# Norm sums carried through the residual update: added on VectorE, rooted as token columns, spread back by a matmul

## The reference

```python
def rms(x):
    xf = x.astype(jnp.float32)
    return (xf * lax.rsqrt(jnp.mean(xf * xf, axis=-1, keepdims=True) + EPS)).astype(x.dtype)
def modulate(h, shift, scale):
    return h * (1 + scale) + shift
def swiglu(h, wi, wo):
    g, u = jnp.split(h @ wi, 2, axis=-1)
    return (jax.nn.silu(g) * u) @ wo
```

## Time and profile before

| | us |
|---|---|
| median of three runs | 3114.03 |
| the profiled execution, its own time | 3109.35 |
| its span | 3107.6 |
| PE matmul busy | 2909.2 (94%) |
| DVE busy | 1670.3 (54%) |
| ACT busy | 1223.8 (39%) |
| POOL busy | 250.8 (8%) |

### The profile page before, as it was taken

How to read it: one execution, slowest core, us unless ns; L and a number is a source line. 1 busy time by engine, 2 the same in 40 slices (tenths; PEclk the granted TensorE clock), 3 DMA queues, 4 the chain that set the end, 5 groups by cost and what they waited for, 6 DMA issues and landing times.

```text
span 3107.6 us, 47235 instructions
## 1 busy us (share of the span) xinstructions
PE 2909.2 (94%) x16044; PEld 2390.0 (77%) x16044; DVE 1670.3 (54%) x2799; ACT 1223.8 (39%) x1983; POOL 250.8 (8%) x163
## 2 busy tenths in 40 slices
PE   6799998999889999899998889999799899999999
PEld 2488886764478888788886369997699899888888
DVE  0433325956443332433327546558669877677765
ACT  1322223335332222322224445445545455455444
POOL 0100002200010000100003000000028400000000
PEclk8799999999899999999999899999999999999999
DMA  7422221237222222222222344553156555566654
GB/s 290 163 100 96 95 101 69 74 128 292 95 81 95 101 95 102 81 94 96 100 102 82 136 154 159 182 203 123 69 177 213 174 172 174 186 241 240 243 206 142
DMA packets 144828, 444.84 MB, mean 143 GB/s; under 512 B 16089, under 2 KB 44889, under 8 KB 144225
## 3 DMA queue, kind: packets, MB, share of 16 engines
q1 hardware_dynamic: 112896, 409.51, 37.8%
q10 hardware_dynamic: 31840, 34.13, 3.1%
HBM read 428.37 MB, written 15.20 MB: 143 GB/s over the span
## 4 chain that ended last, share of the span: by engine, by line
PE 84%; DVE 8%; DMA 3%; ACT 2%; issue 1%; POOL 1%; SPq 0%; ACTq 0%; DVEq 0%
PE bank L1385 20%; PE bank L1386 20%; PE bank L1387 20%; PE bank L1756 11%; DMA raw<-w_stream_dram 3%; PE bank L1412 2%; PE bank L1728 2%; PE bank L1576 1%; PE bank L1617 1%; DVE stage_rs L875 1%; PE bank L1423 1%; PE bank L1450 1%; DVE cand L1186 1%; PE bank L1608 1%; PE bank L1588 1%
## 5 line engine op out<-in xcount | busy, mean ns | idle before, releaser
L1385 PE MATMUL bank<-H,w_hi 128*128 128x256 f32 (+1 forms) x3232 | 1093.2, 338 | 64.9 <-DVE H L866 58.4
L843 DVE TENSOR_TENSOR w_lo<-raw,w_hi 128x1024 fp32r<-128x1024 f32 x584 | 714.7, 1225 | 685.3 <-ACT w_hi L435 676.3
L1386 PE MATMUL bank<-H,w_hi 128*128 128x256 f32 (+1 forms) x3232 | 1068.0, 330 | 0.0
L1387 PE MATMUL bank<-H,w_lo 128*128 128x256 f32 (+1 forms) x3232 | 1067.4, 330 | 0.0
L435 ACT ACTIVATE w_hi<-raw 128x1024 fp32r<-128x1024 f32 x628 | 660.1, 1052 | 239.1 <-PE bank L1387 208.3
L1385 PEld LDWEIGHTS bank<-H,w_hi 128*128 128x128 f32 x3232 | 623.3, 193 | 136.4 <-issue 71.8
L1386 PEld LDWEIGHTS bank<-H,w_hi 128*128 128x128 f32 x3232 | 623.4, 193 | 59.5 <-issue 5.6
L1387 PEld LDWEIGHTS bank<-H,w_lo 128*128 128x128 f32 x3232 | 622.5, 193 | 54.9
L1385 PE MATMUL bank<-act_hi,w_hi 128*128 128x512 f32 (+1 forms) x704 | 263.8, 375 | 0.0
L1387 PE MATMUL bank<-act_hi,w_lo 128*128 128x512 f32 (+1 forms) x704 | 255.5, 363 | 0.0
L1386 PE MATMUL bank<-act_lo,w_hi 128*128 128x512 f32 (+1 forms) x704 | 255.5, 363 | 0.0
(11 more groups left out here) (207 smaller groups left out, 2775.8 us busy)
## 6 DMA issues: line engine op xcount, KB each, us to landing
raw<-w_stream_dram SPq DMA_DIRECT2D x772, 512.0 KB, 3.3
gelu_scratch<-gelu ACTq DMA_DIRECT2D x108, 128.0 KB, 3.5
gelu_in<-gelu_scratch ACTq DMA_DIRECT2D x108, 128.0 KB, 3.4
bias<-bias_in_dram ACTq DMA_DIRECT2D x1, 3072.0 KB
X<-x_in_dram SPq DMA_DIRECT2D x1, 2048.0 KB, 13.8
mem<-mem_in_dram SPq DMA_DIRECT2D x1, 1024.0 KB, 9.9
rope<-rope_in_dram ACTq DMA_DIRECT2D x2, 512.0 KB
sub<-sub_in_dram ACTq DMA_DIRECT2D x1, 1024.0 KB
```

The costliest lines, as they stand in the source:

```text
L843: nc.vector.tensor_tensor(w_lo[:, s, :], raw[:, s, :], w_hi[:, s, :].bitcast(F32), ALU.subtract).then_inc(lo_ready, 1)
L1385: nc.tensor.matmul(to, w_hi[:, s, cut], hi, start=first, stop=False, skip_group_check=True)
L1386: nc.tensor.matmul(to, w_hi[:, s, cut], lo, start=False, stop=False, skip_group_check=True)
L1387: return nc.tensor.matmul(to, w_lo[:, s, cut], hi, start=False, stop=last, skip_group_check=True)
```

## The change

Three things, in all seven norms with carried sums.

First, the squares of the eight chunks are no longer multiplied by `ones` one by one. ACT writes the first square to `x_sq_sum` (in `stage_rs`) and the others to two buffers in turn; DVE adds the squares of chunks 1 to 6 to it (`add_square`), the one of chunk m-1 between the split and the update of row `m`. Square 7 is not added. The loops of these rows are written out on all three engines, and PE waits for `x_done` before it reuses a bank.

Second, at the end PE takes the sum and the last square as stationary operands, one block of 128 tokens at a time, against two columns of `ones`: the sums then stand with tokens on the partitions, 8 columns (LC) or 4 (L). ACT roots these columns, DVE inverts them, and PE multiplies a broadcast of each column with the identity into bank 5, which gives the inverse root of every token on all partitions. DVE multiplies `X` by that bank. The tiny Sqrt that loads the table stands ahead of the eight rows.

Third, in the norms with a shift, DVE itself makes the modulated chunks 0, 3 and 6, which POOL made, and takes the low part one chunk behind, which was two.

```diff
+DVE_Y = (0, 3, 6)
+        x_sq_sum = stage_rs[:, 0, :]
+        x_root = tiny[:, 48:56]
+        x_sums_bank, x_rows_bank = bank[4], bank[5]
...
@@ ACT, norm
-                link(nc.scalar.activation(tiny[:, 9:10], tiny[:, 0:1], ACT.Sqrt))
                 if n["summed"]:
                     act.wait_ge(x_sums_ready, n["update"] + 1)
-                    root(0)
+                    some = slice(0, 2 * blocks_of(hv))
+                    nc.scalar.activation(x_root[:, some], x_sums_bank[:, some], ACT.Sqrt, bias=tiny[:, 0:1]
+                                         ).then_inc(rs_ready, 1)
@@ ACT, ffn (project_out alike, with one split a row)
+                sqrt_table()
+                for m in range(KC):
+                    for k in range(WO_T):
+                        split(t1 + WO_T * m + k + AHEAD)
+                    squares(update, halves, m)
@@ DVE, norm
+                    if n["summed"]:
+                        some = x_root[:, 0:2 * blocks_of(hv)]
+                        nc.vector.reciprocal(some, some).then_inc(x_inverse_ready, 1)
+                        dve.wait_ge(x_rows_ready, n["update"] + 1)
+                        rs = x_rows_bank
...
+                        if n["summed"]:
+                            if c >= 1:
+                                low(c - 1)
+                            if n["shift"] is not None and y_by_dve(n, c):
+                                dve.wait_ge(z_ready, n["chunk_at"] + c + 1)
...
+                                    ins = nc.vector.tensor_scalar(stage_y[:, c % 2, some], z_buf(c)[:, some],
+                                                                  n["scale"](c, half), n["shift"](c, half), ALU.mult,
+                                                                  ALU.add)
@@ DVE, new
+            def add_square(update, halves, m):
+                dve.wait_ge(x_sq_ready, KC * update + m + 1)
+                if m >= 2:
+                    dve.wait_ge(x_sq_added, (KC - 2) * update + m - 1)
+                w = width(halves)
+                nc.vector.tensor_tensor(x_sq_sum[:, 0:w], x_sq_sum[:, 0:w], stage_sq[:, m % 2, 0:w], ALU.add
+                                        ).then_inc(x_sq_added, 1)
@@ DVE, project_out
+                for m in range(KC):
+                    split(FIRST[stage] + m + AHEAD)
+                    if m >= 2:
+                        add_square(number, halves, m - 1)
+                    dve.wait_ge(tile_used, FIRST[stage] + m + 1)
...
@@ PE: open_x_sums and x_sum go
+            def close_x_sums(update, halves):
+                count = blocks_of(halves)
+                def sums_of(squares, first):
+                    for j in range(count):
+                        ins = nc.tensor.matmul(x_sums_bank[:, 2 * j:2 * j + 2], squares[:, j * P:(j + 1) * P], ones[:, 0:2],
+                                               start=first and j == 0, stop=not first,
+                                               skip_group_check=True)
+                    return ins
+                pe.wait_ge(x_sq_added, (KC - 2) * (update + 1))
+                sums_of(x_sq_sum, True)
+                pe.wait_ge(x_sq_ready, KC * (update + 1))
+                sums_of(stage_sq[:, (KC - 1) % 2, :], False).then_inc(x_sums_ready, 1)
+                pe.wait_ge(x_inverse_ready, update + 1)
+                for j in range(count):
+                    ins = nc.tensor.matmul(x_rows_bank[:, j * P:(j + 1) * P],
+                                           x_root[:, 2 * j:2 * j + 1].to_broadcast([P, P]), ident, start=True, stop=True)
+                ins.then_inc(x_rows_ready, 1)
```

More of the change, by code:

```diff
@@ L293, in z_buf, with blocks_of, y_by_dve, y_count @@
             return (stage_z if c % 4 < 2 else stage_raw)[:, c % 2, :]
-        def sq_buf(q, i):
-            return stage_sq[:, q, :] if q < 2 else stage_raw[:, 0, :] if q == 2 else stage_z[:, i, :]
+        x_sq_sum = stage_rs[:, 0, :]
+        x_root = tiny[:, 48:56]
+        x_sums_bank, x_rows_bank = bank[4], bank[5]
+        def blocks_of(halves):
+            return 2 * len(halves)
+        def y_by_dve(n, c):
+            return n["summed"] and c in DVE_Y
+        def y_count(n, c):
+            return n["shifted_at"] + sum(not y_by_dve(n, k) for k in range(c + 1))
         def norm_done(name):
@@ L521, in ffn @@
                     chunks(i)
-                with act.Fori(0, 2) as i:
-                    for q in range(4):
-                        for k in range(WO_T):
-                            split(t1 + WO_T * q + k + AHEAD, i, 4 * WO_T)
-                        squares(update, halves, i, q)
+                sqrt_table()
+                for m in range(KC):
+                    for k in range(WO_T):
+                        split(t1 + WO_T * m + k + AHEAD)
+                    squares(update, halves, m)
             def project(stage):
@@ L632, in project_out @@
             def project_out(stage, halves, update):
-                with act.Fori(0, 2) as i:
-                    for q in range(4):
-                        split(FIRST[stage] + q + AHEAD, i, 4)
-                        squares(update, halves, i, q)
+                sqrt_table()
+                for m in range(KC):
+                    split(FIRST[stage] + m + AHEAD)
+                    squares(update, halves, m)
             act.wait_ge(in_loaded, 32)
@@ L1073, in attend, with project_out @@
                     split(t)
-            def project_out(stage, gate, halves):
-                with dve.Fori(0, 2) as i:
-                    for q in range(4):
-                        m = 4 * i + q
-                        split(FIRST[stage] + q + AHEAD, i, 4)
-                        dve.wait_ge(tile_used, FIRST[stage] + q + 1 + 4 * i)
-                        for half in range(len(halves)):
-                            scalar = sm("one") if gate is None else mod[:, gate, bass.ds(5 * KC + m, 1), half]
-                            ins = update(m, half, bank[4 + q][:, half * NT:(half + 1) * NT], scalar)
-                        ins.then_inc(x_done, 1)
+            def project_out(stage, gate, halves, number):
+                for m in range(KC):
+                    split(FIRST[stage] + m + AHEAD)
+                    if m >= 2:
+                        add_square(number, halves, m - 1)
+                    dve.wait_ge(tile_used, FIRST[stage] + m + 1)
+                    for half in range(len(halves)):
+                        scalar = sm("one") if gate is None else mod_col(gate, 5, m, half)
+                        ins = update(m, half, bank[4 + m % 4][:, half * NT:(half + 1) * NT], scalar)
+                    ins.then_inc(x_done, 1)
             nc.vector.memset(zeros[:, :], 0.0)
@@ L1162, in _ @@
             norm("og_c")
[L1163 removed]
+            project_out("out_c", None, "L", 6)
             norm("ffn_c")
@@ L1491, in ffn @@
                 pe.wait_ge(a_ready, FC * f + FC - 1)
-                open_x_sums()
-                with pe.Fori(0, 2) as i:
+                for i in range(2):
                     for q in range(4):
+                        if i:
+                            pe.wait_ge(x_done, KC * update + q + 1)
                         for kk in range(WO_T):
```

97 lines of the change are left out of this document (47 added, 50 removed).

## The result

The changed kernel took 3065.12 us (median of four runs, 3062.47 to 3072.09), the kernel before beside it 3115.43 (four runs, 3108.86 to 3120.34): a ratio of 0.9853, 95% interval 0.9835 to 0.9872. The prediction was 3070.0, in a range of 3055 to 3088. The profiled execution took 3066.56 us, 42.8 less than the 3109.35 of before; its span was 3064.7 us, 42.9 less than 3107.6.

What follows compares the result with a forecast made beforehand. It took three bounds by place: PE in feed-forward rows, short-step chains in norms, the update-square-split circle in out stages. Terms 15.7 + 3.1 + 4.5 + 15.6 + 1.9 + 0 - 0.5 = 40.3 us gave 3069.1, named 3070, range 3055 to 3088.

Steps and rivals of the forecast that it cites:

- Rows of the feed-forward parts: Feed-forward 0 to 3: PE never pauses, so dropped products win 15.7 us in the first three, 3.1 in the last.
- the opening product and the five others: Each LC feed-forward part: six products with `ones` on PE's path, 0.87 us each, 5.2 us in all.
- that 0.36 in mix_c: mix_c: the last addition comes 0.36 us late, counted within the norm's new path; 1.9 us won there.
- out_a, out_b, out_c: Update-square-split circle sets the pace: out_a wins 4.5 us; out_b with post1 gives 0, out_c with ffn_c loses 0.5.
- The norms: Four LC norms: last update to PE's restart falls from 11.5 to 7.1 us, 4.4 won each, 17.6 in all.
- the chunk made by DVE: LC norms: the modulated chunk that POOL made in 2 us becomes 0.7 on DVE.
- The 0.5 a norm that I took off: Four LC norms: allowance for PE's lower clock in the new tail, leaving 15.6 us of 17.6.
- the clock stays up: Rival, restarts: shorter pauses never lower PE's clock, so 12 us more won, 3058 us; chance 0.12.
- The tail at half clock: Rival, LC and L norms: short products run at 1.2 GHz, 10 us less won, 3079 us; chance 0.16.
- The table: ACT's root table: a load costs the profile row's 1.28 us, without the skill's 1.38 drain, worth 6 us more.
- slower: Rival, 42 additions: each waits for ACT's square and delays the circle; 3125 us and more; chance 0.05.
- the rows' gain: Rival, feed-forward rows: written-out rows make PE wait, so the 15.7 + 3.1 are lost, 3088 us; chance 0.07.

Runs made afterwards that it cites:

- e8: The kernel before, with only its six two-pass loops over the rows written out on ACT, DVE and PE: 3105.11 us, ratio 0.9989.
- e1: The changed kernel with the norms' sums, root and inversion 512 wide again and no spread: 3083.7 us, ratio 0.991.
- e3: The changed kernel with the root table's load back in the norm, behind the last square: 3070.18 us, ratio 0.9866.
- e4: The changed kernel, but in out_a, out_b, out_c DVE adds behind the update, except the last addition: 3063.18 us, ratio 0.9844.
- e5: The changed kernel, but in out_a, out_b, out_c ACT squares each row behind the next row's split: 3055.01 us, ratio 0.9829.
- e6: The changed kernel with useless 512-wide products filling PE's pauses in the four LC norms: 3058.45 us, ratio 0.984.
- e9: The changed kernel with the edits of e5 and e6 together, plus fills in post1 and ffn_c: 3043.57 us, ratio 0.9792.
- e10: The changed kernel measured again, unedited, beside the same runs of the kernel before as e9: 3065.43 us, ratio 0.9853.
- e2: The changed kernel with every modulated chunk made by POOL, none by DVE: 3066.53 us, ratio 0.9862.
- e7: The wide-sums kernel of e1, but inverted roots written to PSUM and all modulated chunks made by POOL: 3080.99 us, one run.

## Why the prediction was right

The steps held by place, and the sum of the terms (40.3) came out at 42.9. The agreement is better than the parts: the feed-forward parts gave 1.2 more than their terms, out_a 0.5, the norms 1.2, and unchanged code, which alone moves a span by 7 us, added nothing in the first profile by luck.

*Rows of the feed-forward parts.* Right, e8 and e1 show it alone: the products with `ones` go, the additions never wait. It was 18.2 instead of 15.7. Counted in feed-forward 1, the opening product and the five others gave 5.4 us, where 5.2 was costed; 0.6 more comes from the first fifteen products behind the shorter norm, and the rest, some 0.3, I did not split. Feed-forward 3 won 3.0 by its products, where 3.1 was costed, and lost 0.3 to the first addition, which makes one step of its updates 8.26 in place of 7.92; the prediction had that 0.36 in mix_c. Its first hundred products took 0.9 longer, a cost that the prediction left out. The profiles show where it comes from: PE waits there for `w_lo` and goes on 11.62 to 11.63 us behind the restart in the changed kernel, e3, e4, e5, e6, e9 and e10, whatever it did before (it had idled from 0.07 to 2.75 us). In the kernel before, the same product began 10.75 behind the restart. The split for it waits on ACT behind the norm's chunks, the copy of `mem` and the table load; ACT began it 8.38 us behind PE's restart before and 9.25 now, because PE's restart moved up by more than ACT's work did. With all chunks on POOL (e2) the product began 10.72 behind it. The shorter norm thus lost part of its gain at the next wait.

*out_a, out_b, out_c.* Right: PE's work there was worth nothing once the circle led. Steps of 4.26 and 3.38 stood just under the 4.3 to 4.4 and 3.4 to 3.6 that were named, and out_b lost 0.6 to its first update (0.4) and 1.1 in its rows (1.3). post1 took 5.64, above the 4.5 to 5.4 named, and won 1.4 instead of 2. e4 shows the addition on the circle, e8 the 0.1 of the register instructions, and e5 that in out_b and out_c the circle sets the pace.

*The norms.* The size was right (7.36 against 7.1), its division was not. I gave the chunk made by DVE 1.3 us; in the changed kernel e2 gives it 0.17. The cause is POOL: beside rows in PSUM it makes the first chunk in 1.1 us instead of 2.0 (e7), so the two edits take away the same wait, and either alone would nearly have done. post0 shows it, which never had a table load in its path: 11.12 us before, 9.79 with the rows in SBUF and the chunk on DVE (e1), 9.97 with the rows in PSUM and every chunk on POOL (e7). Some 0.2 of each difference is the writing out (e8). The 1.3 is near what the first of the two edits wins, and 0.17 what the second adds. The narrow columns are worth 2.44 (e1; with POOL making the chunks, 9.97 in e7 against 7.53 in e2, the same), the early load 0.7 to 0.8 where the clock holds (e3). The spread took 1.16 (1.05), the multiplication from PSUM 0.69, no longer than from SBUF.

*The clock.* The 0.5 a norm that I took off did not come: all narrow products of the LC tails ran at 2.4 GHz (1.05 and 1.16), also between pauses of 0.84 and 0.59 us. What the rows had shown behind pauses of 5 and 9 us did not carry over to these short ones. Without the 2 us taken off the sum would have been 42.3, which is nearer. Nor did the rival "the clock stays up": after 2.96 us of pause the first products took 0.63 us, as they had after 9.04. e6 shows what that rival would have been worth, about 1.9 in feed-forward 1 and in 2. "The tail at half clock" fell for LC, but e3 caught it in post0, at 1.35, and in part in mix_b. In post1 and ffn_c the sums did run at half clock, behind 4.6 and 7.3 us of pause, as the forecast had it.

*The table.* The row was kept, and e3 bears it out: no load shows the drain. (Five drains of 1.38 would have made 6.9, not the 6 that the prediction gave.)

*The other rivals.* No addition waited for a square, so "slower" had nothing to stand on; the rows' gain arrived.

Left open: why the clock holds among the narrow products in one tail and falls in another. It is not PE's order alone: in mix_b the same program lost it in e6 and kept it in e9, and post0 kept it in the changed kernel and lost it in e3.

## What to carry to other kernels

Cost a change stage by stage with the wait that ends last there: the same removed products won 5.4 us in a feed-forward part, where PE led, and nothing where a circle over two in-order engines led. There an instruction's place in the order (a square behind the split, not ahead of it) was worth 7 to 13 us over three stages. Before a shorter chain is credited to one edit, look whether another edit takes away the same wait: here moving an operand to PSUM and giving the chunk to VectorE each took away the wait for GpSimd, and the second of them added 0.17 us. Follow a won wait to the next one: feed-forward 3 gave 0.9 us back at a weight tile whose split had not moved up as far. Compare stretches, not spans, when unchanged code alone moves the span by 7 us, and ratios, not medians, when runs come from two chips.

## What the hardware did that I had not expected

GpSimd's modulated chunk of 128x512 took 2.0 us beside multiplications with both operands in SBUF and 1.1 beside ones with an operand in PSUM, which is no more than beside an idle VectorE (0.56 a half).

Useless products in a pause of 2.96 us kept the granted clock at 1.00 and made the restart 1.9 us faster; but in post0 of e9 the clock fell while PE went from whole products to sums and fills, busy for 6.97 of 7 us, and the same tail in mix_b lost the clock in one execution (e6) and kept it in another (e9).

A sum over 128 partitions by 128x2 products, eight instructions in 1.05 us, and a spread by 128x128 products in 1.16, took, with the root and inversion of 8 columns, 2.44 us less than sums, root and inversion 512 wide, of which the inversion alone is 3.35.
